# The last expert's down product in another PSUM bank, expert 14's scatter between its two halves, high scatter products ahead of the low ones, and the residual by TensorE for one tile of rows

## The reference

```python
proj = x @ w_in[l]
heads_out = concat(gla_mixer(...), ssd_mixer(...), rwkv7_mixer(...))
x = layer_norm(ALPHA * x + heads_out @ w_out[l], ln1_g[l], ln1_b[l])
ffn = sum over 16 experts e of gate[:, e] * ((silu(x @ w_gate[e]) * (x @ w_up[e])) @ w_down[e])
x = layer_norm(ALPHA * x + ffn, ln2_g[l], ln2_b[l])
```

## Time and profile before

| | |
|---|---|
| Median of 3 launches | 903.29 us (901.61 to 903.34) |
| Profiled execution | 903.42 us, its span 901.6 us |
| PE busy | 846.2 us, 94% of the span |
| DVE busy | 317.2 us, 35% |
| ACT busy | 178.8 us, 20% |
| Bytes moved | 245.85 MB, mean 273 GB/s |
| Mean granted TensorE clock | 0.976 |

### The profile page before, as it was taken

The page is one execution under the profiler, slowest core; times in us unless marked ns, Lnnn a source line. Parts: engine busy times, 40 slices in busy tenths (PEclk is TensorE's granted clock), DMA queues, the critical chain, the costliest instruction groups (busy, mean ns, idle before and its releaser), DMA issues. The chain is left out here.

```text
span 901.6 us, 12941 instructions
## 1 busy us (share of the span) xinstructions
PE 846.2 (94%) x5423; PEld 472.6 (52%) x5423; DVE 317.2 (35%) x657; ACT 178.8 (20%) x373; POOL 25.9 (3%) x102
## 2 busy tenths in 40 slices
PE   8999999989999999999699998999799999999993
PEld 8888666455334443333288866654543344433331
DVE  1296447373111111111234955282802211111114
ACT  1132323222101120000222233241320012100001
POOL 7100000000000000000000000000000000000000
PEclk9999999989999999999999999999899999999997
DMA  8944201078999989999934522020989999799981
GB/s 271 355 147 170 94 3 66 29 310 345 349 423 421 421 341 388 422 420 421 387 100 165 187 95 95 2 94 13 421 323 370 422 421 420 307 423 421 422 371 50
DMA packets 54227, 245.85 MB, mean 273 GB/s; under 512 B 8356, under 2 KB 11280, under 8 KB 29584
## 3 DMA queue, kind: packets, MB, share of 16 engines
q1 hardware_dynamic: 52816, 240.20, 67.0%
q0 software_dynamic: 1344, 4.72, 1.4%
HBM read 243.85 MB, written 1.05 MB: 272 GB/s over the span
## 5 line engine op out<-in xcount | busy, mean ns | idle before, releaser
L528 PE MATMUL bank<-ring,xg 128*64 128x512 f32 x576 | 148.8, 609 | 2.9 <-issue 2.0
L1004 PE MATMUL bank<-x_cm,ring 128*128 128x256 f32 x576 | 125.9, 379 | 2.2 <-ACT x_cm L1987 1.4
L1004 PEld LDWEIGHTS bank<-x_cm,ring 128*128 128x128 f32 x576 | 108.9, 190 | 18.4 <-issue 2.1
L528 PE MATMUL bank<-ring_more,xg 128*64 128x512 f32 x384 | 101.8, 596 | 1.2 <-DMA ring_more<-in_exp_w_up 1.2
L748 DVE TENSOR_TENSOR y_lo<-bank,y_hi 128x512 fp32r<-128x512 f32 x32 | 22.1, 692 | 214.7 <-issue 168.9
L528 PEld LDWEIGHTS bank<-ring,xg 128*64 128x64 f32 x576 | 44.6, 139 | 77.9 <-issue 75.9
L558 PE MATMUL bank<-ring,x_cm 128*64 128x512 f32 x336 | 80.0, 617 | 0.7 <-DVE g_col L724 0.7
L733 DVE TENSOR_SCALAR x_cm<-bank,g_col 128x512 f32<-128x512 f32 x32 | 24.0, 751 | 101.4 <-PE bank L528 85.7
L1011 PE MATMUL bank<-ring,x_cm 128*128 128x512 f32 x128 | 57.7, 599 | 0.0
L681 ACT ACTIVATE y_hi<-bank 128x512 fp32r<-128x512 f32 x32 | 19.1, 598 | 192.7 <-PE bank L558 192.7
L528 PEld LDWEIGHTS bank<-ring_more,xg 128*64 128x64 f32 x384 | 31.0, 137 | 49.8 <-issue 48.2
(11 more groups left out here) (379 smaller groups left out, 952.8 us busy)
## 6 DMA issues: line engine op xcount, KB each, us to landing
ring<-in_exp_w_down SPq DMA_DIRECT2D x42, 1024.0 KB, 11.8
ring<-in_exp_w_gate SPq DMA_DIRECT2D x38, 1024.0 KB, 12.0
ring<-in_exp_w_up SPq DMA_DIRECT2D x38, 1024.0 KB, 9.2
ring<-in_w_in SPq DMA_DIRECT2D x24, 1024.0 KB, 7.5
ring_more<-in_exp_w_gate SPq DMA_DIRECT2D x24, 1024.0 KB, 15.0
ring_more<-in_exp_w_up SPq DMA_DIRECT2D x24, 1024.0 KB, 13.0
ring_more<-in_exp_w_down SPq DMA_DIRECT2D x22, 1024.0 KB, 14.7
ring<-in_w_out SPq DMA_DIRECT2D x8, 1024.0 KB, 6.2
```

The source lines that it names most:

```text
L528: m = T.matmul(b[SL * i:SL * i + SL, :], xg[g][:, 4 * h + k, cols], w[:, k, :], start=(h == 0 and k == 0), stop=(h == 1 and k == 3))
L1004: m = T.matmul(out_, w[:, k, c:c + n], x_cm[:, k, :], start=(k == 0), stop=(k == KD - 1))
```

## The change

Five edits, all in the experts and the second norm:

1. `y_bank`: the down product of the last expert goes to `b_hid[N % 2]`, which is bank 4, in place of bank 7. `down(15)` waits for `v_pick_t` (DVE has read bank 4) in place of the two copies of expert 14.
2. `down` can be issued by halves. At the end PE now does `down(14)`, the first half of `down(15)`, `scatter(14)`, the second half of `down(15)`, the residual, `scatter(15)`.
3. `scatter` does its four products with `y_hi` first, and waits for `y_lo` only then. This holds for every expert.
4. The residual matmuls (L624 before, L665 now) move from ahead of `position_row(15)` to just ahead of `scatter(15)`, and do tile 0 only: 2 matmuls in place of 4.
5. In the second norm, tile 1 gets its residual from DVE: `scalar_tensor_tensor` computes ALPHA * x + bank into `x_tm`, then `bn_stats` reads `x_tm`. `standardize(1)` and `out_half(1, ...)` read `x_tm` too.

```diff
+        def y_bank(n, N):
+            return b_hid[N % 2] if n == N - 1 else b_y
...
-            def down(n):
+            def down(n, parts=(0, 1)):
                 e, r = divmod(n, rounds)
-                pe.wait_ge(*at("v_he", n + 1))
-                if n:
-                    pe.wait_ge(*at("s_yhi", n))
-                    pe.wait_ge(*at("v_ylo", n))
-                for h in range(2):
+                b = y_bank(n, N)
+                if 0 in parts:
+                    pe.wait_ge(*at("v_he", n + 1))
+                    if n == N - 1:
+                        pe.wait_ge(*at("v_pick_t", n))
+                    elif n:
+                        pe.wait_ge(*at("s_yhi", n))
+                        pe.wait_ge(*at("v_ylo", n))
+                for h in parts:
...
             def scatter(n):
                 pe.wait_ge(*at("s_yhi", n + 1))
-                pe.wait_ge(*at("v_ylo", n + 1))
                 pe.wait_ge(*at("v_pick_t", n + 1))
-                for j in range(TT):
-                    for y in (y_hi, y_lo):
+                for y in (y_hi, y_lo):
+                    if y is y_lo:
+                        pe.wait_ge(*at("v_ylo", n + 1))
+                    for j in range(TT):
                         for hf in range(2):
...
-                if n:
+                if 0 < n < N - 1:
                     scatter(n - 1)
...
                 if n == N - 2:
                     hidden(N - 1, 1)
                     turn(N - 1)
-                    pe.wait_ge(*done("v_x1", l))
-                    for j in range(TT):
-                        for hf in range(2):
-                            T.matmul(bank[2 * j + hf][:], ident_a[:], x_tm[:, j, BCOL * hf:BCOL * hf + BCOL],
-                                     start=False, stop=False)
                     position_row(N - 1)
...
-                down(n)
+                if n < N - 1:
+                    down(n)
...
+            down(N - 1, (0,))
+            scatter(N - 2)
+            down(N - 1, (1,))
+            pe.wait_ge(*done("v_x1", l))
+            for hf in range(2):
+                T.matmul(bank[hf][:], ident_a[:], x_tm[:, 0, BCOL * hf:BCOL * hf + BCOL], start=False, stop=False)
             scatter(N - 1)
...
                 def sums(j, hf):
...
+                    if which and j == 0:
+                        c.add(V.bn_stats(bn6[:, j, hf, :], bank[hf][:]))
+                    else:
                         cs = slice(hf * 512, hf * 512 + 512)
                         do(V.scalar_tensor_tensor(out=x_tm[:, j, cs], in0=x_tm[:, j, cs], scalar=ALPHA,
-                                                  in1=bank[4 + 2 * hf + j][:], op0=ALU.mult, op1=ALU.add))
+                                                  in1=bank[2 * j + hf if which else 4 + 2 * hf + j][:],
+                                                  op0=ALU.mult, op1=ALU.add))
                         c.add(V.bn_stats(bn6[:, j, hf, :], x_tm[:, j, cs]))
```

More of the change, by code:

```diff
@@ L557, in down @@
                         for hf in range(2):
-                            m = T.matmul(b_y[SL * hf:SL * hf + SL, :], he[n % 2][:, fb, :], w[:, 2 * (fb % 2) + hf, :],
+                            m = T.matmul(b[SL * hf:SL * hf + SL, :], he[n % 2][:, fb, :], w[:, 2 * (fb % 2) + hf, :],
                                          start=(fb == 0), stop=(fb == FB - 1))
@@ L680, in y_high @@
                     act.wait_ge(*at("t_scat", n))
-                mark(A.activation(y_hi[:], b_y[:], ACT.Copy), "s_yhi")
+                mark(A.activation(y_hi[:], y_bank(n, N)[:], ACT.Copy), "s_yhi")
             if rounds == 1:
@@ L747, in y_low @@
                     dve.wait_ge(*at("t_scat", n))
-                mark(V.tensor_tensor(y_lo[:], b_y[:], y_hi[:].bitcast(F32), ALU.subtract), "v_ylo")
+                mark(V.tensor_tensor(y_lo[:], y_bank(n, N)[:], y_hi[:].bitcast(F32), ALU.subtract), "v_ylo")
             def turned_pick(n):
@@ L1507, in sums @@
                         dve.wait_ge(*done("t_mix", l, 2 * j + hf + 1))
+                    else:
+                        dve.wait_ge(*done("t_scat", l))
+                    if which and j == 0:
+                        c.add(V.bn_stats(bn6[:, j, hf, :], bank[hf][:]))
+                    else:
                         cs = slice(hf * 512, hf * 512 + 512)
                         do(V.scalar_tensor_tensor(out=x_tm[:, j, cs], in0=x_tm[:, j, cs], scalar=ALPHA,
-                                                  in1=bank[4 + 2 * hf + j][:], op0=ALU.mult, op1=ALU.add))
+                                                  in1=bank[2 * j + hf if which else 4 + 2 * hf + j][:],
+                                                  op0=ALU.mult, op1=ALU.add))
                         c.add(V.bn_stats(bn6[:, j, hf, :], x_tm[:, j, cs]))
-                    else:
-                        dve.wait_ge(*done("t_scat", l))
-                        c.add(V.bn_stats(bn6[:, j, hf, :], bank[2 * j + hf][:]))
                     if hf:
@@ L1523, in standardize @@
                     dve.wait_ge(*done("s_rstd", l, 2 * which + j + 1 + (which * j if l < L - 1 else 0)))
[L1524 to L1532, removed]
                     inc(V.tensor_scalar(x_tm[:, j], x_tm[:, j], bn2[:, j, 0:1], bn2[:, j, 1:2], ALU.subtract, ALU.mult), "v_z")
@@ L1547, in out_half @@
                     dve.wait_ge(*done("s_rstd", l, 2 * which + j + 1 + (which * j if l < L - 1 else 0)))
-                    do(V.scalar_tensor_tensor(out=x_tm[:, j, cs], in0=bank[2 * j + hf][:], scalar=bn2[:, j, 0:1],
+                    do(V.scalar_tensor_tensor(out=x_tm[:, j, cs], in0=x_tm[:, j, cs] if j else bank[hf][:], scalar=bn2[:, j, 0:1],
                                               in1=ln_vec[:, 0, cs], op0=ALU.subtract, op1=ALU.mult))
```

## The result

The changed kernel takes 896.71 us, median of 6 launches (894.03 to 898.97), against 902.99 us (901.61 to 903.34) in the same measurement: ratio 0.9935, 95% interval 0.9914 to 0.9956. Two more measurements, each on a chip of its own, gave 0.9898 (0.9871 to 0.9925) and 0.9906 (0.9889 to 0.9922). So it is faster, by 0.4 to 1.3%; the forecast was 894.2 us, 1.0%. The profiled execution took 895.41 us with a span of 893.6 us, 8.0 us less than before in both.

The account below looks back on a forecast made before the run. PE, busy 94% of the span, was taken as the bound, with waits at the end of each layer's experts. From 903.42 us, - 5.35 - 5.35 + 1.55 = -9.15 gave 894.3, or 894.2 for a median; range 891.8 to 897.2.

Parts of the forecast that it names:

- PE's tail: End of each layer's experts, from residual or position_row to the norm: 11.29 us against 16.64, 5.35 us less per layer.
- both waits: PE standing still about 1.79 us behind the copies of expert 14, and the same again for expert 15, in each layer.
- the row of lengths 3.44, 1.72, 1.13, 1.72, 1.76: Predicted PE order: down(14), first half of down(15), scatter(14), second half, one tile's residual, in us.
- DVE in layer 1: Second norm, tile 1: four new DVE instructions take 2.82 us against 1.27, 1.55 us more; bounds 1.37 and 1.63.
- Tile 1 in layer 0: Layer 0's norm: the same 1.55 us on tile 1 is covered, with 1 us of room; cost 0.
- The restart: PE's first transposes after layer 0's experts: moves by 5.35 us with the jump; taken as 0, with -1.4 below.
- PE waits for its instructions: Reading of 1.38 us before PE's transposes in layer 0, in which no semaphore is missing.
- The weights: Loads for down(15) arrive with 1.6 to 2 us left; rival: they become the wait, 901.8 us, chance 0.03.
- The order in the scatter: All 32 scatters, high products first: taken as 0; 3 us above if the middle wait opens the stream anew.
- The clock: Half-clock drop at layer 0's norm and three other short drops in layer 1: taken as 0, +/-1 us.
- the fetch that does not move: Rival: PE restarts in layer 0 at 451.23 as before, that layer's gain is gone, 899.6 us; chance 0.09.
- the wait within the scatter: Rival: PE runs dry mid-scatter in all 32 scatters, 0.36 us each, 11.5 us, 905.8 us, slower; chance 0.03.

Follow-up runs that it names:

- scatter_behind: Against the changed kernel, expert 14's scatter stands behind both halves of down(15) instead of between them; 894.21 us (4 launches), beside 902.31 for the kernel before.
- swap_bodies: Against the changed kernel, the branch's two bodies change places in every engine's program, so the one that runs stands last; 908.23 us (10 launches).
- warm_tail: Against the changed kernel, ten matmuls into bank 7, which nothing reads, added behind layer 0's last scatter; 898.12 us (10 launches).
- residual_both_by_pe: Against the changed kernel, PE adds both tiles' residual right ahead of the last scatter, with the norm of before; 894.84 us (5 launches).

## Why the prediction was right, and where it was off

- *PE's tail.* Expected 5.35 us less per layer, measured 4.78. The mechanism is the one described: both waits gone, the residual in the place of the second, nothing late. The term that was mis-sized is the row of lengths 3.44, 1.72, 1.13, 1.72, 1.76 taken from `down` and residual by themselves: each change between 64-row, 64-column and full tiles goes with about 0.15 us more (first half to scatter 5.30 in place of 5.16 from `down(14)` on, second half 1.87 for 1.72, residual 1.92 for 1.76), and `turn(15)` to `position_row` takes 0.67 in place of 0.59. The waits of before hid these changes; without them three show. In scatter_behind there is one fewer, and the stretch is 0.17 us shorter. That the shape is the cause is read from these lengths; no run varies it alone.
- *DVE in layer 1.* 1.55 us expected, 1.44 measured.
- *Tile 1 in layer 0.* Covered, as expected, with 0.8 us of room.
- *The restart.* Taken as 0, it gained 0.28 us in the first trace and 0.24 in the second. The reading "PE waits for its instructions" is shown by swap_bodies; that jump and restart move together is shown by the 6.63 to 6.72 us from `y_lo` in eight traces. It also gives the size: `y_lo` is complete 1.61 us ahead of the norm in place of 1.33, 0.28 us more.
- *The weights.* Neither half of `down(15)` waits for its load.
- *The order in the scatter.* 0, as taken.
- *Sum of the traces.* -2 x 4.78 - 0.28 + 1.44 = -8.40; the layers' other stretches give back 0.2 and the last store 0.2, -8.0 in all, against -9.15 forecast.
- *The clock.* The prediction counts three short drops behind the norm's in layer 1; the trace of before has four of 3.4 us each, ahead of the one at the end. Priced at 1 us either way, the clock is the larger uncertainty: single launches lie 5 us apart. The median of the first six fell 2.5 us above the forecast with the half-clock time at 48 us; the next ones lie at 893.80 and 895.15. All three medians lie in the range of 891.8 to 897.2 us, the first by 0.5 us only; 3 of the 16 launches lie above it (898.59 to 898.97 us), so that the first median came out inside is in part luck.

Of the rivals, the fetch that does not move did not happen, the weights are in time, and the wait within the scatter costs nothing.

## What to carry to other kernels

When an engine is busy 94% of the time, look for the end of a phase, where the software pipeline has nothing left to put beside a copy: a free bank and two matmuls that have to be done anyway (the residual), moved into the wait, took 3.2 us of it per layer, and another edit for the same wait, the order in the scatter, then added nothing. When waits are taken away, price what they had hidden, here some 0.15 us at each change of tile shape. With launches that spread by 5 us, compare distances in traces, and compare launches at equal granted clock.

## What the hardware showed beyond that

- With the DMA engines full, PE runs its first instruction behind the jump over the long body 6.7 us after its last wait ahead of it is satisfied (eight traces; 8.1 us in scatter_behind, where the instruction packet took 2.2 us), and stands still for 4.1 to 4.5 us where the jump lies at the start of the experts. Matmuls ahead of the jump delay it (warm_tail), waits that are satisfied early let it go ahead (residual_both_by_pe).
- Each us of TensorE at half clock goes with 0.29 us of time, over 64 launches of three kernels with 23 to 52 us of it.
